# The first block's attention in three steps a unit instead of four, with the two shortest query tiles in one

## What is computed

```python
# fox, 6 heads of 64: a decay by cumulated log forget gates
logits = q @ k.T * scale + c[t] - c[s]
p = softmax(where(causal, logits, -inf)); o = p @ v
# diff, 4 heads of two 32-wide maps
a = softmax(q1 @ k1.T) - lam * softmax(q2 @ k2.T)     # causal
o = rms_norm(a @ v) * (1 - lam_init)
# dsa, 6 heads of 64 on one shared k and v: only the 128 best causal keys of each query
score = sum_h w[t, h] * relu(q_idx[t, h] . k_idx[s])
_, sel = top_k(where(causal, score, -inf), 128)
o = softmax(q @ k[sel].T * scale) @ v[sel]
```

## Time and profile before

| what | us |
|---|---|
| median of 3 runs (2233.62 to 2236.26) | 2233.86 |
| the profiled execution, its own time | 2233.64 |
| its span | 2231.7 |
| PE busy | 2178.9 (98%) |
| DVE busy | 1263.0 (57%) |
| ACT busy | 901.3 (40%) |
| POOL busy | 291.8 (13%) |

### The profile page before, as it was taken

How to read it: one execution, slowest core, us unless ns; L and a number is a source line. 1 busy time by engine, 2 the same in 40 slices (tenths; PEclk the granted TensorE clock), 3 DMA queues, 4 the chain that set the end, 5 groups by cost and what they waited for, 6 DMA issues and landing times.

```text
span 2231.7 us, 31549 instructions
## 1 busy us (share of the span) xinstructions
PE 2178.9 (98%) x12794; PEld 1786.5 (80%) x12794; DVE 1263.0 (57%) x1751; ACT 901.3 (40%) x1574; POOL 291.8 (13%) x215
## 2 busy tenths in 40 slices
PE   7999999999999999999999999999999999999998
PEld 6886688778888776688778888989888887888777
DVE  5687648983224687648984226422666636212794
ACT  3447843222213447843222223232565524212673
POOL 3001213121222001322121000000010000000230
PEclk9999999999999999999999999999999999999999
DMA  5220016543563220016543321132000122321221
GB/s 164 90 71 2 1 57 207 173 148 86 143 176 93 90 71 1 2 59 205 182 145 81 138 96 58 49 98 75 16 23 9 53 76 92 123 70 57 72 72 57
DMA packets 149107, 194.28 MB, mean 87 GB/s; under 512 B 43165, under 2 KB 96426, under 8 KB 148962
## 3 DMA queue, kind: packets, MB, share of 16 engines
q1 hardware_dynamic: 110288, 169.83, 23.3%
q10 hardware_dynamic: 38514, 22.26, 3.7%
q0 software_dynamic: 160, 0.16, 0.0%
HBM read 180.51 MB, written 11.72 MB: 86 GB/s over the span
## 4 chain that ended last, share of the span: by engine, by line
PE 90%; DVE 4%; ACT 3%; issue 2%; DMA 0%; ACTq 0%; POOLq 0%; DVEq 0%
PE ps L535 69%; PE ps L2757 3%; PE ps L1890 3%; PE ps L2774 2%; PE ps L2786 2%; PE ps L2304 1%; PE ps L2261 1%; PE ps L2290 1%; DVE probs_t L2105 1%; PE ps L2762 1%; PE ps L1924 1%; ACT probs_t L2863 1%; DVE neg_max L2072 1%; PE ps L542 1%; PE ps L2760 1%
## 5 line engine op out<-in xcount | busy, mean ns | idle before, releaser
L500 DVE TENSOR_TENSOR w_low<-w_raw,w_high 128x2048 fp32r<-128x2048 f32 (+4 forms) x140 | 303.4, 2167 | 487.5 <-ACT w_high L495 487.3
L495 ACT ACTIVATE w_high<-w_raw 128x2048 fp32r<-128x2048 f32 (+4 forms) x140 | 253.2, 1809 | 577.2 <-PE ps L535 560.6
L535 PE MATMUL ps<-h_hi,w_high 128*128 128x512 f32 (+1 forms) x1168 | 439.7, 376 | 3.1 <-DVE w_low L500 2.1
L535 PE MATMUL ps<-h_lo,w_high 128*128 128x512 f32 (+1 forms) x1168 | 437.2, 374 | 0.0
L535 PE MATMUL ps<-h_hi,w_low 128*128 128x512 f32 (+1 forms) x1168 | 436.7, 374 | 0.0
L535 PEld LDWEIGHTS ps<-h_hi,w_high 128*128 128x128 f32 x1168 | 219.9, 188 | 53.9 <-issue 10.7
L535 PEld LDWEIGHTS ps<-h_hi,w_low 128*128 128x128 f32 x1168 | 219.8, 188 | 39.6
L535 PEld LDWEIGHTS ps<-h_lo,w_high 128*128 128x128 f32 x1168 | 220.0, 188 | 39.1 <-issue 0.5
L535 PE MATMUL ps<-w_high,h_hi 128*128 128x512 f32 (+3 forms) x576 | 214.2, 372 | 0.6 <-DVE h_lo L3159 0.6
L535 PE MATMUL ps<-w_low,h_hi 128*128 128x512 f32 (+3 forms) x576 | 211.6, 367 | 0.0
L535 PE MATMUL ps<-w_high,h_lo 128*128 128x512 f32 (+3 forms) x576 | 211.4, 367 | 0.0
(11 more groups left out here) (389 smaller groups left out, 3681.6 us busy)
## 6 DMA issues: line engine op xcount, KB each, us to landing
w_raw<-in_w_gate_up SPq DMA_DIRECT2D x44, 1024.0 KB, 5.2
ada_w<-in_ada_w SPq DMA_DIRECT2D x24, 1024.0 KB, 5.2
w_raw<-in_w_down SPq DMA_DIRECT2D x20, 1024.0 KB, 4.8
w_raw<-in_w_in SPq DMA_DIRECT2D x16, 1024.0 KB, 5.1
w_raw<-in_c_in_w SPq DMA_DIRECT2D x16, 1024.0 KB, 5.7
w_raw<-in_w_out SPq DMA_DIRECT2D x8, 1024.0 KB, 4.8
w_raw<-in_ab_in_w SPq DMA_DIRECT2D x8, 1024.0 KB, 5.1
masked_scratch<-mask_table ACTq DMA_DIRECT2D x8, 512.0 KB, 3.5
```

The lines of the kernel that those rows point to most:

```text
L495: e.activation(w_high[j % 2][:, 0:size], w_raw[j % 2][:, 0:size], ACT.Copy).then_inc(sig.w_high_done, 1)
L500: e.tensor_tensor(w_low[j % 2][:, 0:size], w_raw[j % 2][:, 0:size], w_high[j % 2][:, 0:size].bitcast(F32), ALU.subtract).then_inc(sig.w_lo ...
L535: mm = e.matmul(dst, lhs, rhs, start=start and a == 0, stop=stop and a == 2)
```

## The change

The four steps of a unit become three: query tiles 1 and 0 are one step of 256 + 128 columns in one bank for each member, tiles 2 and 3 are a step each. Instead of 40 steps there are 30, and the three pairs of banks are now fixed to the three steps. The loop runs over units, in two halves. TensorE does, in unit u: scores of step 3u, the transposes of the two last steps of unit u - 1 in a row, a bank-7 event, values of the first step of unit u - 1, the second event, scores of steps 3u + 1 and 3u + 2, the transposes of step 3u, the wide event of unit u - 1, and the values of its last two steps in a row. In the step of two lengths the short tile's scores, mask and gates come first, then those of the long one. ScalarE exponentiates the four pieces of that step one by one and signals each member apart, copies all 384 columns of both members at once, and `probs_t1` has three buffers. VectorE takes the maxima of step 3u, the inverse of unit u - 1 and a share of the rounds in the first half, the maxima of the other two steps and a share of the rounds in the second; the shares are the same 37 rounds over 15 halves. The last iteration does both `pair_finish` before the last `invert`.

```diff
-            AHEAD, SETS = 2, 3
-            ROUND_STEPS = 30
+            TILES = ((1, 0), (2,), (3,))
+            PER = len(TILES)
+            ROUND_HALVES = 15
...
+                for u in range(-1, self.U + 1):
+                    inside, events = 0 <= u < self.U, self.first_half[u]
+                    if inside:
+                        scores(3 * u)
+                        masks(3 * u)
...
+                    if u > 0:
+                        turn_probs(3 * u - 2)
+                        turn_probs(3 * u - 1)
+                    for kind, i in events[0:1]:
+                        event(kind, i)
...
+                    if u > 0:
+                        values(3 * u - 3)
+                    for kind, i in events[1:]:
+                        event(kind, i)
...
+                    if inside:
+                        for s in (3 * u + 1, 3 * u + 2):
+                            scores(s)
+                            masks(s)
...
+                    if inside:
+                        turn_probs(3 * u)
+                    if u > 0:
+                        wide(u - 1)
+                        values(3 * u - 2)
+                        values(3 * u - 1)
...
+                    if u > 1:
+                        copy_o(u - 2)
+                    if u > 0:
+                        copy_probs(3 * u - 2)
+                        copy_probs(3 * u - 1)
+                    for i in turned[0:1]:
+                        copy_turned(i)
+                    if inside:
+                        exps(3 * u)
...
+                    if inside:
+                        exps(3 * u + 1)
+                        copy_probs(3 * u)
+                    if u > 0:
+                        copy_wide(u - 1)
+                    if inside:
+                        exps(3 * u + 2)
...
+                for h in range(2 * self.U + 1):
+                    u = h // 2
+                    if h == 2 * self.U:
+                        for c in range(2):
+                            pair_finish(c)
+                        invert(u - 1)
+                        break
+                    if h % 2 == 0:
+                        maxima(3 * u)
+                        if u:
+                            invert(u - 1)
+                    else:
+                        maxima(3 * u + 1)
+                        maxima(3 * u + 2)
+                    share = min(rounds, early + (rounds - early) * (h + 1) // self.ROUND_HALVES)
```

More of the change, by code:

```diff
@@ L2717, in group, with parts, size, both @@
                     dst = {"q": q_turned[g % 2], "k": k_turned[g % 2], "d": kd_turned}[which]
-                    self.turns.append((first - self.AHEAD - len(chunks) + c, dst, src, g))
+                    self.turns.append((first - 1, dst, src, g))
             def final(self, u):
-                return NT * u + NT - 1
+                return self.PER * (u + 1) - 1
             def bank(self, s, m):
-                return 2 * (s % self.SETS) + m
-            def both(self, s, n):
+                return 2 * (s % self.PER) + m
+            def parts(self, s):
+                at_ = 0
+                for t in self.steps[s][1]:
+                    yield t, at_, (t + 1) * P
+                    at_ += (t + 1) * P
+            def size(self, s):
+                return sum((t + 1) * P for t in self.steps[s][1])
+            def both(self, s, a, n):
                 b = self.bank(s, 0)
-                return ps[:, b:b + 2, 0:n]
+                return ps[:, b:b + 2, a:a + n]
             def spare_bank(self, e, B, event):
@@ L2744, in turn, with added @@
                     mm.then_inc(sig.qk_bank, 1)
+                def added(s, m, t, a, w, start, stop):
+                    u, tiles = self.steps[s]
+                    out_ = ps[:, self.bank(s, m), a:a + w]
+                    if self.units[u].kind == "dsa":
+                        at_ = a if t == 0 else 0
+                        return e.matmul(out_, ident_r[:], keep_mask[:, tiles[0], at_:at_ + w], start=start, stop=stop)
+                    return e.matmul(out_[:, w - P:w], ident_r[:], causal_r, start=start, stop=stop)
@@ L2746, in scores, with gated @@
+                def gated(s, m, t, a, w, stop):
+                    h = 2 * self.units[self.steps[s][0]].n + m
+                    return e.matmul(ps[:, self.bank(s, m), a:a + w], gate_sel[:, h * P:(h + 1) * P], gate_t[:, 0:w], start=False, stop=stop)
                 def scores(s):
-                    u, t = self.steps[s]
-                    x, n = self.units[u], (t + 1) * P
-                    if t == 0:
+                    u, tiles = self.steps[s]
+                    x, parts = self.units[u], list(self.parts(s))
+                    if s % self.PER == 0:
@@ L2758, in scores @@
-                    for m in range(2):
-                        if x.kind == "dsa":
-                            mm = e.matmul(ps[:, self.bank(s, m), 0:n], ident_r[:], keep_mask[:, t, 0:n], start=False, stop=True)
-                        else:
-                            mm = e.matmul(ps[:, self.bank(s, m), t * P:n], ident_r[:], causal_r, start=False, stop=x.kind != "fox")
+                    first = len(parts) == 2
+                    for t, a, w in reversed(parts):
+                        for m in range(2):
+                            e.matmul(ps[:, self.bank(s, m), a:a + w], q[x.rows(m), t * P:t * P + P], k[x.rows(m), 0:w], start=True, stop=False)
+                        if first and t == 0:
+                            for m in range(2):
+                                added(s, m, *parts[1], False, x.kind != "fox")
+                            if x.kind == "fox":
+                                for m in range(2):
+                                    gated(s, m, *parts[1], True)
@@ L2763, in scores, with masks @@
+                def masks(s):
+                    u, tiles = self.steps[s]
+                    x, part = self.units[u], next(self.parts(s))
+                    if x.kind == "dsa" and x.n == 0:
+                        e.wait_ge(sig.keep_ready, B["keep_ready"] + tiles[0])
+                    for m in range(2):
+                        mm = added(s, m, *part, False, x.kind != "fox")
                     if x.kind == "fox":
                         for m in range(2):
-                            h = 2 * x.n + m
@@ L2766, in scores @@
-                            mm = e.matmul(ps[:, self.bank(s, m), 0:n], gate_sel[:, h * P:(h + 1) * P], gate_t[:, 0:n], start=False, stop=True)
+                            mm = gated(s, m, *part, True)
                     mm.then_inc(sig.scores_ready, 1)
                 def turn_probs(s):
-                    u, t = self.steps[s]
-                    e.wait_ge(sig.probs_ready, B["probs_ready"] + s + 1)
                     for m in range(2):
-                        for kt in range(t + 1):
-                            mm = e.transpose(ps[:, self.bank(s, m), kt * P:(kt + 1) * P],
-                                             probs1[s % 3][:, m, kt * P:(kt + 1) * P], ident)
+                        e.wait_ge(sig.probs_ready, B["probs_ready"] + 2 * s + m + 1)
@@ L2776, in turn_probs @@
+                        for b in range(self.size(s) // P):
+                            mm = e.transpose(ps[:, self.bank(s, m), b * P:(b + 1) * P],
+                                             probs1[s % 3][:, m, b * P:(b + 1) * P], ident)
                     mm.then_inc(sig.probs_turned, 1)
                 def values(s):
-                    u, t = self.steps[s]
+                    u, tiles = self.steps[s]
                     x = self.units[u]
                     e.wait_ge(sig.turned_second, B["turned_second"] + s + 1)
-                    if t == 0 and u:
+                    if s % self.PER == 0 and u:
```

168 lines of the change are left out of this document (74 added, 94 removed).

## The result

The changed kernel takes **2242.5 us** (median of 5 runs, 2242.23 to 2243.14) for 2233.86 before; the ratio is 1.0038, with a 95% interval of 1.0027 to 1.0049. It is slower by 8.6 us, where 2230.1 had been forecast and 2225.5 to 2234.5 given as the range.

The account below looks back on a forecast made before the run. TensorE was taken as the bound, with VectorE without slack in units 5 and 6. Terms 0.6 -1.4 -1.7 -0.1 +0.7 = -1.9 us a layer, -3.8 in two, gave 2230.1 us; range 2225.5 to 2234.5.

Parts of the forecast that it names:

- 10.5 + 2.2 = 12.7: Unit 7: 10.5 us of TensorE's own work plus a new 2.2 wait of the 512-wide mask for the last kept set.
- 1.7 us of TensorE idle: End stretch: spreading transposes wait for the last inverse, queued behind both finishing multiplications, and for GpSimd; bounds 1.0 to 2.2.
- Slower: Rival, chance 0.16: grouped rounds hold the maxima, TensorE waits in units 3 to 7; 0.2 more per round gives 2239.3 us.
- The first unit: Unit 0: unit 1's first scores wait for the 0.81 copy, 0.95 exposed where 0.3 was; +0.6 us a layer.
- Units 5 and 6: Diff units set by VectorE's time: 11.15 and 11.5, together 22.65 us for 22.73, -0.1 a layer.
- Units 3, 4 and 7: Units 3 and 4 together 21.0 us for 22.73 (-1.7); unit 7 12.7 with its kept-set wait.
- the starts: Value runs on TensorE: two fewer starts in each unit, 2 x 0.18 us less.
- the operand change: Two score matmuls a unit directly following a mask or gate: 0.1 us each taken, bounds 0 and 0.16.
- Fox units: Units 1 and 2: 13.15 -0.68 -0.35 +0.3 = 12.45 us each, together -1.4 a layer.
- unit 9 with the end: Unit 9 at 12.1 us and the end stretch at 7.7, up to the output product.
- The wait of 0.36 before a fox unit's second turn: Units with two turns: second turn waits for ScalarE's queued copy of the first, 2.5 against 2.2 us, so 0.3.
- The rival that rounds in a row cost nothing: Free rounds, chance 0.05: VectorE needs 10.85 in units 5 and 6, unit 7's wait nearly goes; 2226.4 us.

Follow-up runs that it names:

- e_fill: Changed kernel plus harmless fp32 matmuls where TensorE idled long (four in unit 5, four before unit 7's 512-wide mask, three at the end); 2234.09 us, ratio to before 0.9997.
- e_swap_fill: e_fill with ScalarE's copy of the first group's turned probabilities put ahead of the second group's exponentials in every unit; 2242.95 us, ratio 1.0043.
- e_best: Changed kernel with top-k rounds dealt out by VectorE's idle times, e_end's order at the end and five fillers in unit 0; 2218.91 us, ratio 0.9933.
- e_end: Changed kernel with only the end reordered: last inverse before the two finishing multiplications, last two value runs before the spreading transposes; 2233.77 us, ratio 1.0002.
- e_front: Changed kernel with the 37 top-k rounds dealt out earlier, 3 to each of the first seven half-units, 2 to the next eight; 2230.55 us, ratio 0.9982.
- e_norounds_after: Changed kernel without the 37 top-k rounds during the attention, for timing only; 2223.24 us, ratio 0.9951.
- e_norounds_before: Kernel before the change without the same 37 top-k rounds, for timing only; 2233.67 us, ratio 0.9999.

## Why the prediction was wrong

**The step that failed is one that is not in it: what idle time does to TensorE's clock.** The prediction read the clock of 1.00 in the earlier trace rows, took it as given, and priced each wait at its own length: "10.5 + 2.2 = 12.7" for unit 7, "1.7 us of TensorE idle" at the end. The slower work behind a wait is a term that it put at nothing without a reason. It forecast these two waits well, 2.39 and 1.72 measured. A third was in its numbers without being called one: unit 5 at 11.15 for 9.6 of TensorE's own work is 1.5 us of idle time before unit 6, and 2.28 was measured. At each of the three the clock fell to half for some microseconds. By e_fill that is 8.4 us of the 12.4 between 2230.1 and 2242.5.

None of its rivals has the clock either. "Slower" gave 2239.3 for another reason. Half of its mechanism is there, since TensorE did wait for the copy that stands behind the held exponentials (e_swap_fill). But its price, a dearer round, is refuted: rounds in a row stand at 1.73 and 1.74, as the forecast had them (the earlier trace rows has 1.73). That 2239.3 lies near the measured time is luck.

**Most of the other 4.0 us are terms of the sum.** With the clock up (e_fill) the first layer is 124.26 us instead of the forecast's 122.3, and the second 123.77, together 3.4 more. In the first:

- *The first unit*, forecast +0.6, is +1.07. The wait of 0.99 was forecast as 0.95. Left out was the rule that the prediction had itself worked out for units with two turns: the second turn waits for the copy of the first, and unit 0 has two turns as well. It waits 0.69 there.
- *Units 5 and 6*, forecast 22.65, are 23.65 with the clock up. The five rounds and four reduces of unit 5 are what was forecast; the two small instructions of the inverse are not 0.4 but 0.78 in unit 5 and 0.59 in unit 6 (the last section shows what held them), and the slack of 0.35 that unit 5 was to inherit from unit 4 was not there. VectorE's timeline in after from unit 5's first reduce on, where 1.73 and 1.74 are seen as well:

```profile
218.82 1.01 DVE L2978 TENSOR_REDUCE neg_max<-ps 128x2 f32<-128x512 f32 x2
219.75 0.19 DVE L2986 RECIPROCAL sums_inv<-sums 128x8 f32<-128x8 f32 x1
219.98 0.64 DVE L2991 TENSOR_SCALAR sums_inv<-sums_inv,lam 128x4 f32<-128x4 f32 x1
220.53 0.68 DVE L2642 MAX8 top<-score 128x8 f32<-128x512 f32 x1
...
222.26 0.70 DVE L2642 MAX8 top<-score 128x8 f32<-128x512 f32 x1
...
224.00 0.69 DVE L2642 MAX8 top<-score 128x8 f32<-128x512 f32 x1
...
225.51 2.08 DVE L2978 TENSOR_REDUCE neg_max<-ps 128x2 f32<-128x768 f32 x2
```

- *Units 3, 4 and 7*, forecast 33.7 together, are 34.16 with the clock up.

**What held.** A fox unit without its waits is 12.08 us (12.44 less 0.36) where it was 12.47 (13.15 less 0.68): the runs save 0.39 for the forecast's 0.35. Which part of this is the starts and which the operand change was not taken apart. Fox units are 12.44 and 12.43 for 12.45, unit 8 is 10.51 for 10.6, and unit 9 with the end 19.89 for 19.8 once the clock is up. The wait of 0.36 before a fox unit's second turn was forecast as 0.3, partly by luck: the pieces named for it, 0.81 + 1.02 + 0.60 less overlaps of 0.1 and with 0.1 to start, come to 2.2 or 2.3 and not to the 2.5 that was written, and against 2.2 of TensorE's work they leave 0.1 at most. In after it is 2.43 from the start of the first copy to the second turn. VectorE is the bound from unit 4 on, and the kept set the late one in unit 7. The rival that rounds in a row cost nothing falls. The Trainium skill, VectorE: DVE Perf Modes, The DRAIN you can't avoid, says that a semaphore between operations costs nothing extra, measured on eight copies. The prediction held 1.73 for 1.51 against this, but the two rows do not test it: the next instruction waits on a semaphore in both. What differs is that a search needs the scores that were just replaced, and a reduce does not. No run here takes the semaphores away.

The range was too narrow for the same reason. Both of its bounds were reached by changing terms of the sum, and every new wait was treated as a cost of one time its length. A forecast that has TensorE idle for 2.2 us at one place and 1.7 at another, in a kernel where until then its longest wait in these units was 0.4, had left the region in which its rows were measured.

What was not shown: how much of a unit's growth the longer inverse on VectorE accounts for by itself. It was read from traces and not undone by a run.

## What to carry to other kernels

When a change takes ten short waits of the bound engine and makes three long ones of them, the sum of the waits is not the price: ask of each wait of a microsecond or more what runs behind it, and price that work at half the clock as a case of its own. Before a change that groups work on the main engine, look at what the second engine has interleaved with it: here the grouping was worth 6.0 us a layer with the rounds out of the way, and alone it lost 8.6 us in all. With the rounds laid into VectorE's own idle times (3 before the first maximum, 1 between two maxima), the other order at the end and five fillers, it won 14.8 (e_best against the kernel before beside it), and with the turns moved as well 18.7. Where a wait can't be removed, harmless matmuls in it keep the clock up, if they cover it: in e_swap_fill 2.10 us of idle time were left beside the fillers, and the clock fell.

## What the runs showed of the hardware

**The granted clock fell behind waits of 2 us and less, and not each time.** All ten waits of 1.9 us and more in these attentions went with a fall (before unit 6 and in unit 7 of after and e_end in both layers, in unit 7 of e_swap_fill). The waits of 1.63 and 1.64 before unit 4 did in three of four cases, the wait of 1.72 at the end in two of six (both layers of after, neither of e_front nor of e_norounds_after), the two waits of 0.77 and 0.61 in e_swap_fill's unit 9 in one layer of two, the wait of 0.99 before unit 1 once in fourteen. Outside the attentions, a wait of 0.60 for the same copy, between 1529 and 1558 us, stands in all eleven profiles, and the clock fell behind it in two (e_fill and e_swap_fill). Within each group but the first the instructions next to the wait are the same. The Trainium skill, TensorE: Matmul & The Clock Gate, Part 1: The HAM clock gate, says that the hardware judges by a clock of its own, not by the kernel's instructions, and that the moment of a switch differs from run to run; these mixed counts agree with it.

**The work behind the wait pays.** In the 3-us stretch with the wait before unit 6 of after the clock still reads 1.00. Worked out from stretches of 1 us, the seventeen falls in the attentions began between 0.5 us before TensorE went on and 2.4 us behind that; only two lie inside the wait. A fall cost 1.3 to 1.6 us where a unit can be compared with and without it: 13.77 for 12.44, 21.37 for 19.89, 12.68 for 11.04. A table of busy time hides this: TensorE is as busy in after (120.73) as before, and only the clock's column tells that part of it is the same work done slowly.

**A small instruction on VectorE waited for GpSimd.** The multiplication of four elements behind the reciprocal (L2991, L2929 in before) always has the same shape. It lasts 0.23 us in all 16 cases of before and e_norounds_before, and up to 1.11 in the changed kernels. Two of them in after, with what GpSimd does at the time:

```profile
219.98 0.64 DVE L2991 TENSOR_SCALAR sums_inv<-sums_inv,lam 128x4 f32<-128x4 f32 x1
219.31 1.28 POOL L3074 TENSOR_TENSOR wide<-o_raw,wide 128x512 f32<-128x512 f32 x1 [9.58 <-ACT o_raw L2925]
...
232.08 0.27 DVE L2991 TENSOR_SCALAR sums_inv<-sums_inv,lam 128x4 f32<-128x4 f32 x1
231.05 1.26 POOL L3050 TENSOR_TENSOR proj<-wide,fold_part 64x512 f32<-64x512 f32 x1 [9.76 <-ACT fold_part L2932]
```

It ends at 220.62, the GpSimd multiplication at 220.59; then at 232.35 and 232.31. In all eleven profiles, each one that lasts longer than 0.23 ends 0.02 to 0.04 us after a GpSimd multiplication, and in before none of GpSimd's was running. So the new order set this instruction beside GpSimd's work, and that is where the inverse's 0.78 for 0.4 comes from. No run moved GpSimd's work to undo it.
